# Gated linear attention scores from half-chunk products on two 64-column tiles

## The reference

```python
def gla_scan(q, k, v, la, S0):
    def step(Sst, inp):
        qc, kc, vc, lac = inp
        Bc = jnp.cumsum(lac, axis=1)
        diff = Bc[:, :, None] - Bc[:, None, :]
        decay = jnp.exp(jnp.where(tril[None, :, :, None, None], diff, -jnp.inf))
        A = jnp.einsum('bthd,bshd,btshd->btsh', qc, kc, decay)
        o = jnp.einsum('btsh,bshv->bthv', A, vc) + jnp.einsum('bthd,bhdv->bthv', qc * jnp.exp(Bc), Sst)
        BL = Bc[:, -1]
        S_new = jnp.exp(BL)[..., None] * Sst + jnp.einsum('bshd,bshv->bhdv', kc * jnp.exp(BL[:, None] - Bc), vc)
        return S_new, o
```

## Time and profile before

| | before |
|---|---|
| median of 3 runs | 1227.43 us (1225.89 to 1228.27) |
| profiled execution | 1224.0 us, span 1222.2 us |
| mean granted TensorE clock | 0.992 |
| TensorE matmul busy | 1191.3 us, 97% |
| VectorE busy | 753.4 us, 62% |
| ScalarE busy | 385.6 us, 32% |

### The profile page before, as it was taken

One profiled execution on the slowest core, in us unless ns is written; L12 is line 12 of the kernel. 1 busy time (PEld: TensorE's weight loads), 2 busy tenths in 40 slices (PEclk: granted clock), 3 DMA queues, 4 the chain that ended last, 5 costly groups with the idle time before them and its releaser, 6 DMA issues.

```text
span 1222.2 us, 21460 instructions
## 1 busy us (share of the span) xinstructions
PE 1191.3 (97%) x9065; PEld 1154.3 (94%) x9065; DVE 753.4 (62%) x1427; ACT 385.6 (32%) x515; POOL 2.3 (0%) x7
## 2 busy tenths in 40 slices
PE   8999999999999999999999999999999999999996
PEld 7999998889999998898999999999999999999995
DVE  6732566757878876555554666667666653323766
ACT  6232233323333432323343232232222321111533
POOL 0000000000000000000000000000000000000000
PEclk9999999999999999999999999999999999999998
DMA  6242111533222256653452452222222133222222
GB/s 213 93 136 93 63 53 53 189 110 112 71 99 97 82 172 210 189 217 118 150 176 91 152 176 72 102 69 94 80 70 104 58 120 136 76 91 94 100 70 78
DMA packets 48768, 138.43 MB, mean 113 GB/s; under 512 B 5364, under 2 KB 24948, under 8 KB 39584
## 3 DMA queue, kind: packets, MB, share of 16 engines
q1 hardware_dynamic: 16296, 89.39, 21.8%
q10 hardware_dynamic: 32376, 47.66, 11.4%
HBM read 113.15 MB, written 23.81 MB: 112 GB/s over the span
## 4 chain that ended last, share of the span: by engine, by line
PE 87%; DVE 5%; issue 4%; ACT 2%; DMA 1%; ACTq 0%; POOL 0%; POOLq 0%; DVEq 0%
PE ps L714 59%; PE ps L720 9%; PE ps L823 5%; PE ps L829 3%; PE aux L1006 2%; PE ps L741 1%; PE aux L968 1%; DMA xT<-in_xT 1%; PE aux L1022 1%; PE aux L931 1%; PE aux L958 1%; PE aux L925 1%; DVE wlo L1067 1%; PE aux L1016 0%; DVE xl L1575 0%
## 5 line engine op out<-in xcount | busy, mean ns | idle before, releaser
L714 PE MATMUL ps<-ahi,whi 128*128 128x288 f32 x1536 | 332.3, 298 | 1.8 <-issue 1.8
L714 PE MATMUL ps<-alo,whi 128*128 128x288 f32 x1536 | 329.7, 296 | 0.0
L714 PEld LDWEIGHTS ps<-ahi,whi 128*128 128x128 f32 x1536 | 247.9, 189 | 6.7 <-issue 3.5
L714 PEld LDWEIGHTS ps<-alo,whi 128*128 128x128 f32 x1536 | 246.2, 188 | 0.0
L1067 DVE TENSOR_TENSOR wlo<-wraw,whi 128x2048 fp32r<-128x2048 f32 (+1 forms) x87 | 187.5, 2155 | 89.0 <-ACT whi L1741 85.0
L1741 ACT ACTIVATE whi<-wraw 128x2048 fp32r<-128x2048 f32 (+1 forms) x87 | 156.4, 1798 | 149.0 <-PE ps L714 104.4
L714 PE MATMUL ps<-ahi,wlo 128*128 128x288 f32 x800 | 171.2, 296 | 0.0
L714 PEld LDWEIGHTS ps<-ahi,wlo 128*128 128x128 f32 x800 | 128.8, 189 | 0.0
L720 PE MATMUL ps<-ahi,wlo 128*128 128x288 f32 x736 | 105.4, 295 | 0.0
L720 PEld LDWEIGHTS ps<-ahi,wlo 128*128 128x128 f32 x736 | 100.6, 189 | 0.0
L714 PE MATMUL ps<-achi,wlo 128*128 128x288 f32 x336 | 72.0, 296 | 0.0
(11 more groups left out here) (370 smaller groups left out, 1731.0 us busy)
## 6 DMA issues: line engine op xcount, KB each, us to landing
wraw<-in_w_in SPq DMA_DIRECT2D x31, 1024.0 KB, 5.0
wraw<-in_w_up SPq DMA_DIRECT2D x21, 1024.0 KB, 4.8
gate_scratch<-stg ACTq DMA_DIRECT2D x32, 288.0 KB, 2.9
gt<-gate_scratch ACTq DMA_DIRECT2D x32, 288.0 KB, 2.9
wraw<-in_w_pgate SPq DMA_DIRECT2D x6, 1024.0 KB, 4.8
wraw<-in_w_down SPq DMA_DIRECT2D x8, 704.0 KB, 4.1
wraw<-in_w_down SPq DMA_DIRECT2D x8, 640.0 KB, 3.8
out_C_s<-st ACTq DMA_DIRECT2D x16, 256.0 KB, 3.0
```

Source lines behind the costliest of these rows:

```text
L714: mm = nc.tensor.matmul(ps[:, t % 2, a, 0:HALF], w, x(k)[:, a * HALF:(a + 1) * HALF], start=f, stop=e)
```

## The change

The scores are built by half chunk. A level with w of 32 or less, and the diagonal, never pairs a key of one half chunk with a query of the other. So each product becomes two for a head, keys of 64 tokens with queries of the same 64 (32 late ones in a level), one on partitions 0 to 63 of the bank and one on 64 to 127. Level w = 64 pairs the first half's keys with the second half's queries, all of them: it becomes one product of 64 by 64 and a plain copy. The rest is gathered in a new tile `attd`, half as wide as `att`, and ScalarE copies its two halves into `att` when the last level is in. One wait is new on VectorE (it zeroes `attd` for the next chunk only after ScalarE has read it, which is signalled by `gat_ready`), and `gout` waits on `gat_ready` in place of `at_ready`.

```diff
-        cmask = put("cmask", [P, 8, P], I8)
+        cmask = put("cmask", [P, 8, P // 2], I8)
+        attd = at("attd", [P, H, P // 2], F32, NMASK)
...
                     for h in range(H):
-                        r, at_ = (slice(0, L), h * L) if c < NC else (half_of(h % 2), h // 2 * TS)
-                        mm = nc.tensor.matmul(b[r, at_:at_ + ln], gk[:, h, t0:t0 + ln],
-                                              gq[:, h, t0:t0 + ln], start=True, stop=True)
+                        for e in range(2) if c < NC else (h % 2,):
+                            at_, t1 = (h * TS, t0 + TS * e) if c < NC else (h // 2 * TS, t0)
+                            mm = nc.tensor.matmul(b[half_of(e), at_:at_ + TS], gk[:, h, t1:t1 + TS],
+                                                  gq[:, h, t1:t1 + TS], start=True, stop=True)
...
+                            if w == TS:
+                                mm = nc.tensor.matmul(b[0:TS, h * TS:(h + 1) * TS], xl[:, h, 0:TS], xl[:, h, TS:],
+                                                      start=True, stop=True)
+                                continue
+                            for e in range(2) if c < NC else (h % 2,):
+                                at_, r = (h * TS // 2, half_of(e)) if c < NC else (h // 2 * TS // 2, half_of(0))
+                                late = xl[:, h, r].rearrange("p (b s) -> p b s", s=2 * w)[:, :, w:]
+                                mm = nc.tensor.matmul(b[half_of(e), at_:at_ + TS // 2].rearrange("p (b s) -> p b s", s=w),
+                                                      xl[:, h, r], late, start=True, stop=True)
...
-                    pe.wait_ge(at_ready, NC + 1 + c + 1)
+                    pe.wait_ge(gat_ready, c + 1)
...
-                    link(V.memset(att[:, :, :], 0.0))
+                    if c:
+                        dve.wait_ge(gat_ready, c)
+                    else:
+                        V.memset(att[TS:, :, 0:TS], 0.0)
+                    link(V.memset(attd[:, :, :] if c < NC else att[:, :, :], 0.0))
...
-                        if c < NC:
-                            i = V.copy_predicated(late(att[:, :, :]), late(bcast(cmask[:, k, :], H, 1)),
-                                                  b[:, 0:H * L // 2].rearrange("p (h b s) -> p h b s", h=H, s=w))
+                        if w == TS:
+                            i = V.tensor_copy(att[0:TS, :, TS:], b[0:TS, 0:H * TS].rearrange("p (h s) -> p h s", h=H))
+                        elif c < NC:
+                            i = V.copy_predicated(late(attd[:, :, :]), late(bcast(cmask[:, k, :], H, 1)),
+                                                  b[:, 0:H * TS // 2].rearrange("p (h b s) -> p h b s", h=H, s=w))
...
-                    if g == (3 if c < NC else 1):
+                    if c < NC and g == 3:
+                        dve.sem_inc(attd_ready, 1)
+                    elif c == NC and g == 1:
                         dve.sem_inc(at_ready, 1)
...
+                elif s[0] == "lev" and s[1] < NC and s[2] == 3:
+                    act.wait_ge(attd_ready, s[1] + 1)
+                    for e in range(2):
+                        i = A.activation(att[half_of(e), :, half_of(e)], attd[half_of(e), :, :], ACT.Copy)
+                    i.then_inc(gat_ready, 1)
```

More of the change, by code:

```diff
@@ L263, in build @@
         ones = put("ones", [P, P])
-        cmask = put("cmask", [P, 8, P], I8)
+        cmask = put("cmask", [P, 8, P // 2], I8)
+        NMASK = where[0]
         nmask = put("nmask", [P, 2, P])
+        attd = at("attd", [P, H, P // 2], F32, NMASK)
         bmask = put("bmask", [P, 4])
@@ L447, in build @@
         at_ready = sem("at_ready")
+        attd_ready = sem("attd_ready")
+        gat_ready = sem("gat_ready")
         c_ready = sem("c_ready")
@@ L941, in _ @@
                     v, wd = (vm, DV + 1) if which == "m" else (vg, DV)
-                    pe.wait_ge(at_ready, (NC + 1) * (1 + (which == "g")))
+                    pe.wait_ge(at_ready, NC + 1 + (which == "g"))
                     pe.wait_ge(blk_ready, q + 1)
@@ L1418, in _ @@
                     R = [x[:, :] for x in rowt]
-                    V.tensor_copy(cmask[:, :, :], cmaskf[:, :, :])
+                    for e in range(2):
+                        V.tensor_copy(cmask[half_of(e), :, :], cmaskf[half_of(e), :, half_of(e)])
                     link(V.memset(rr[:, :], 0.0))
@@ L1592, in _ @@
                     if c < NC:
-                        i = V.copy_predicated(att[:, :, :], bcast(cmask[:, 7, :], H, 1),
-                                              b.rearrange("p (h s) -> p h s", h=H))
+                        i = V.copy_predicated(attd[:, :, :], bcast(cmask[:, 7, :], H, 1),
+                                              b[:, 0:H * TS].rearrange("p (h s) -> p h s", h=H))
                     else:
@@ L1597, in _ @@
                             r = half_of(e)
-                            i = V.copy_predicated(att[r, 0:2, 0:TS], bcast(cmask[r, 7, r], 2, 1),
+                            i = V.copy_predicated(att[r, 0:2, 0:TS], bcast(cmask[r, 7, :], 2, 1),
                                                   b[r, 0:P].rearrange("p (h s) -> p h s", h=2))
@@ L1626, in _ @@
                                 r = half_of(e)
-                                i = V.copy_predicated(late(att[r, 0:2, 0:TS]), late(bcast(cmask[r, k, r], 2, 1)),
+                                i = V.copy_predicated(late(att[r, 0:2, 0:TS]), late(bcast(cmask[r, k, :], 2, 1)),
                                                       b[r, 0:TS].rearrange("p (h b s) -> p h b s", h=2, s=w))
@@ L2054, in _ @@
                 elif s[0] == "gload":
-                    act.wait_ge(at_ready, 2 * (NC + 1))
+                    act.wait_ge(at_ready, NC + 2)
                     for _ in range(NGT):
```

## The result

The changed kernel takes 1219.22 us (median of 4 runs, 1217.90 to 1219.62), the kernel before on the same chips 1227.85 (4 runs, 1225.89 to 1229.13): ratio 0.9935, 95% interval 0.992 to 0.995. The change takes 8.6 us off the medians. The profiled execution took 1219.62 us with a span of 1216.4, for 1224.0 and 1222.2.

A forecast was written before the change was run, and what follows sets the result against it. TensorE was taken as the bound in chunks 1 to 3, VectorE's chain in chunk 0. 3 x (1.91 - 0.1) + 1.25 = 6.7 us off a median of 1227.4 gave 1220.7, range 1216.5 to 1224.8.

The forecast's parts named there:

- The bound: GLA chunks 1 to 3: TensorE's work sets the time, so each microsecond it saves counts unless it must wait.
- The price goes with the weight columns: Score products on TensorE: time follows the weight columns each record loads, not moving columns; 0.106 falls to 0.0275 us a record.
- Levels 32 and narrower: Level stages on TensorE: 0.0275 us a record; a two-level stage of 32 records takes 1.10 us for 1.70, gaining 0.60.
- the rival of long runs at 0.051: Level stages: records beyond the sixteenth slow to 0.051 us; 4.1 us gained in all, 1223.3; chance 0.18.
- Level 64: In `lev 0`: 8 records on one half at 0.084 us, 0.67 in all; the whole stage gains 0.37 us.
- The slower rival: Score products: the two halves don't overlap, records at 0.084 us, 4.15 us more a chunk, 1244.0; chance 0.04.
- The diagonal: Diagonal products on TensorE, each chunk: 16 records take 0.73 us for 0.89, gaining 0.16.
- Edges: Start and end of each half-width run on TensorE: 0.08 us on entering and 0.14 on leaving, 0.22 together.
- VectorE's copies: Masked copies: 0.30 us for 128 elements, 0.46 for levels 2 and 1; 1.4 us saved a chunk, diagonal 0.28 of it.
- The hop: ScalarE's two copies before the score products: 0.73 us plus some 0.1 for signals; TensorE waits 0.1 a chunk.
- Chunk 0: First GLA chunk, set by VectorE's chain: last copy ends about 1.3 us earlier, gain 1.25 us.

The follow-up runs named there:

- few_cols: Kernel before, each level's product keeping 128 weight columns but only 32 moving columns for 64, part of the scores left out: 1226.02 us in one run.
- grouped: Changed kernel with diagonal and narrow-level products all on the bank's first half, then all on the second: 1222.84 us, ratio 0.9979 to the kernel before.
- diag_full: Changed kernel with the diagonal back at four 128 by 128 products per chunk, placed by two masked copies: 1218.39 us in one run.
- hop2: Changed kernel with ScalarE's two copies into the score tile done twice: 1224.03 us in one run.
- lev64_turns: Changed kernel with level 64's products on the two bank halves by turns and two VectorE copies for one: 1219.01 us in one run.
- lev_first: Changed kernel with the last level's copy ahead of the last tile's work on VectorE and ScalarE: 1218.38 us in one run.
- combo3: Changed kernel with key transposes before the diagonal and level 64 on the halves by turns: 1219.78 us (median of 6), ratio 0.9945 to the kernel before.
- combo4: combo3 with ScalarE's score copies ahead of the last level, which VectorE writes into `att` by two copies: 1219.54 us (median of 6), ratio 0.9945.
- combo5: combo3 with five products of constants filling TensorE's first wait in chunk 0: 1219.20 us (median of 6), ratio 0.9943 to the kernel before.
- trans_first: Changed kernel with the key transposes ahead of the diagonal, so half-width products form one stretch: 1218.31 us in one run.

## Why the prediction was right

The forecast was 1220.7, the median 1219.2. By the profile I said 6.7 us and the four chunks show 7.1. Step by step:

- *The bound.* Right: in chunks 1 to 3, what TensorE saves is the time. The table below adds up to what the chunk gained.
- *The price goes with the weight columns.* Right for 128 columns of weights, and few_cols is the proof: half the moving columns, 1.70 us as before. With 64 on one half it is right only in part: grouped has 0.039 us with 32 moving columns and 0.049 with 64.
- *Levels 32 and narrower.* The rate came out, records 0.029 apart to the end for 0.0275, and the rival of long runs at 0.051 fell. The stage is 1.06 us start to start, but the predicted 1.10 held the entry too. With the 0.12 that the main products beside it lose it is 1.18, and the gain 0.52 for 0.60.
- *Level 64.* Mis-sized. I took 0.084 a record from two records on one half; seven records show (0.62 - 0.228) / 6 = 0.065. That is 0.15 us of what `lev 0` gained beyond the 0.37. That the group of two held an edge is likely, and not shown.
- *The slower rival* stood on the same 0.084. grouped, which has no turns, is the nearest case to it, and it loses 4.2 us by the chunks against the changed kernel, where the rival had 23 (1244.0 against 1220.7). Even without turns the change would have gained.
- *The diagonal.* Predicted 0.16; together with its transposes 0.12 in chunk 1, and 0.11 and 0.14 by chunks 1 and 2 of diag_full.
- *Edges.* I had them at 0.08 in and 0.14 out from one row each. They come to more: the exit also shows in the first main pair (0.37 us for 0.34), and full-width transposes between half-width products take 0.59 for 0.44.
- *VectorE's copies.* Predicted 0.44 for the diagonal, 0.30 for 128 elements and 0.46 for levels 2 and 1; measured 0.44 and 0.30, and level 1 0.44.
- *The hop.* Predicted 0.73 and signals, measured 0.84 for the pair. Its wait was put at 0.1 a chunk, and in chunk 1 none shows (1.83, as in grouped). That is luck of size and not slack: in hop2 0.84 more costs 0.84.
- *Chunk 0.* Predicted 1.25, measured 1.31. Counted from each chunk's start, the last copy starts at 34.12 us before and at 33.14 after, and takes 0.36 for 0.64, so its end gains 1.26; the scores start 1.09 sooner (34.47 us in, for 35.56), 0.16 less than the mechanism said. The other 0.22 comes in the products behind, which the sum didn't have.

| us, chunk 1 | gain predicted | gain measured |
|---|---|---|
| diagonal and transposes | 0.16 | 0.12 |
| `lev 0` | 0.37 | 0.66 |
| `lev 1` and `lev 2` | 1.20 | 1.28 |
| `lev 3` | 0.18 | 0.25 |
| four runs of main products | in the stages | -0.44 |
| state products, hop, scores | -0.10 | 0.03 |
| sum | 1.81 | 1.90 |

So the sum of a chunk is nearer than its terms, and that is luck: level 64 and the hop were priced too dear, the edges too cheap.

The clock was not in the sum. It was at 1.00 in both profiled kernels over this stretch, so it didn't matter, but lev64_turns, lev_first, combo3, combo4 and few_cols all had a lower clock (a mean of 0.57 to 0.71 over 292 to 296 us) behind the same wait in chunk 0. The cleanest price is few_cols, whose chunk 0 took 1.48 us more than that of the kernel before; both had waited 0.89, and the kernel before kept its clock. The other four came out 0.9 to 1.6 us longer than the changed kernel there, with other causes mixed in; three of them had a second wait of 0.36 us, but combo5 had one of 0.35 and kept its clock. What decides it stays open: no run here gives a wait length that separates the two. The Trainium skill, TensorE: Matmul & The Clock Gate, Part 1, the section on 56 ns, has a floor of 25 ns for a matmul; the rate by turns, 0.029, agrees with it. The Trainium skill, TensorEngine Tiling (Array Packing), Key Properties, has a drain at a change of tiling mode. The transposes at 0.59 for 0.44 agree.

Also open is how much of a half-clock stretch falls into the timed runs as opposed to the profiled ones. It may be why combo5's 0.7 us isn't seen, but that is only argued.

## What to carry to other kernels

When a small float32 product costs the same for 32 and 64 moving columns, cut the weight columns and let the halves take turns: two records of 64 columns by turns on the halves of a bank took 0.058 us for one of 0.106, and 0.078 without turns. Put the narrow products next to each other: each change of width cost about 0.1 us here. Count the edges on the neighbours too, since the price of a stage start to start left out 0.12 us that the main products paid. And count what the other engines pay in the same edit: here two half copies on VectorE for one would have turned 7 us of gain into a loss of 4 (1.7 of it in the stretch with the lower clock), and the gathering tile on the idle engine is what kept it. Take rates from long runs, not from the one pair that the trace happens to have.

## What the runs showed that I had not expected

- Records on one half of the bank, without turns: 0.039 us with 32 moving columns (grouped); with 64 moving 0.049 (grouped, 16 records, one change of half among them) and 0.065 in a short run of seven.
- A masked copy on 64 partitions costs as one on 128: four of 128 elements 1.53 us, two 0.77.
- The same wait of about 1.1 us in front of TensorE leaves the granted clock at 1.00 in one kernel's execution and is followed by a mean of 0.57 over four microseconds in another's (the changed kernel and lev64_turns); trans_first and combo3 part in the same way behind 1.25 us, the kernel before and few_cols behind 0.89. Ten recorded products of constants in that wait went with a clock of 1.00, in the one execution profiled.
- In chunk 0 the eight score products take 1.80 us to the next tile in one kernel and 2.15 in another, by how VectorE's copies of the state fall between them (the changed kernel, and diag_full or combo5).
